# Turning old rows and scaled new rows into one sum at three boundaries of a four-stage transformer kernel

## The reference, cut to what matters

```python
def rms_norm(x, g):
    return x * rsqrt(mean(x * x, -1) + EPS) * g

def conv_ffn(x, w_up, conv_w, conv_b, w_down):        # FFN_HIDDEN = 2816
    u = x @ w_up
    c = conv_b + sum(conv_w[j] * shifted(u, j - 1) for j in range(3))   # over tokens
    g, val = split(c)
    return (gelu(g) * val) @ w_down

a = mixer(rms_norm(h, g0));     h = h + rms_norm(a, g1)
f = conv_ffn(rms_norm(h, g2));  h = h + rms_norm(f, g3)
```

## Time and profile before

| what | value |
|---|---|
| median of three runs | 1057.07 us |
| the profiled execution | 1056.94 us |
| its span in the trace | 1055.1 us |
| PE busy | 1026.9 us, 97% |
| DVE, ACT, POOL busy | 63%, 53%, 40% |
| granted PE clock, mean | 0.999 of full speed |

### The profile page before, as it was taken

How to read it: one execution, slowest core, us unless ns; L and a number is a source line. 1 busy time by engine, 2 the same in 40 slices (tenths; PEclk the granted TensorE clock), 3 DMA queues, 4 the chain that set the end, 5 groups by cost and what they waited for, 6 DMA issues and landing times.

```text
span 1055.1 us, 21644 instructions
## 1 busy us (share of the span) xinstructions
PE 1026.9 (97%) x8138; PEld 941.0 (89%) x8138; DVE 667.6 (63%) x1094; ACT 557.1 (53%) x1014; POOL 418.1 (40%) x283
## 2 busy tenths in 40 slices
PE   9999999999999999999999999999999999999997
PEld 7788699999978888699999987899999999999996
DVE  4555867767767766777676766766676555554445
ACT  5655665555564654665555556644543455554442
POOL 1000243334333443433343363865653375533331
PEclk9999999999999999999999999999999999999999
DMA  9334456566434443365655624333213245446551
GB/s 354 102 120 140 159 182 206 188 201 191 151 138 160 156 135 128 124 210 184 201 191 167 205 77 160 104 119 120 81 62 121 81 140 157 151 135 215 195 181 42
DMA packets 46284, 161.82 MB, mean 153 GB/s; under 512 B 5264, under 2 KB 6544, under 8 KB 46096
## 3 DMA queue, kind: packets, MB, share of 16 engines
q1 hardware_dynamic: 45072, 156.79, 44.7%
q0 software_dynamic: 1152, 4.19, 1.2%
HBM read 159.91 MB, written 1.05 MB: 153 GB/s over the span
## 4 chain that ended last, share of the span: by engine, by line
PE 89%; DVE 5%; ACT 2%; POOL 2%; issue 1%; DMA 0%; DVEq 0%; SPq 0%; ACTq 0%
PE work L411 13%; PE work L413 13%; PE work L412 13%; PE work L1849 9%; PE acc L411 6%; PE acc L412 6%; PE acc L413 6%; PE work L2567 4%; PE work L2579 3%; PE acc L2579 2%; PE acc L2096 1%; PE acc L2110 1%; PE acc L2112 1%; PE acc L1941 1%; PE work L1387 1%
## 5 line engine op out<-in xcount | busy, mean ns | idle before, releaser
L380 POOL TENSOR_TENSOR low<-raw,high 128x1024 fp32r<-128x1024 f32 x110 | 269.0, 2449 | 276.5 <-ACT high L367 274.0
L380 DVE TENSOR_TENSOR low<-raw,high 128x1024 fp32r<-128x1024 f32 (+1 forms) x185 | 271.0, 1473 | 147.9 <-ACT high L367 147.8
L367 ACT ACTIVATE high<-raw 128x1024 fp32r<-128x1024 f32 (+2 forms) x295 | 298.6, 1026 | 36.6 <-DMA raw<-in_w_out 23.7
L411 PE MATMUL work<-xh,high 128*128 128x256 f32 (+1 forms) x1032 | 290.0, 281 | 2.1 <-DVE v_sb L1534 1.7
L412 PE MATMUL work<-xl,high 128*128 128x256 f32 (+1 forms) x1032 | 287.9, 279 | 0.0
L413 PE MATMUL work<-xh,low 128*128 128x256 f32 (+1 forms) x1032 | 287.8, 279 | 0.0
L411 PEld LDWEIGHTS work<-xh,high 128*128 128x128 f32 (+1 forms) x1032 | 193.2, 187 | 9.0 <-issue 5.6
L412 PEld LDWEIGHTS work<-xl,high 128*128 128x128 f32 (+1 forms) x1032 | 193.3, 187 | 1.7
L413 PEld LDWEIGHTS work<-xh,low 128*128 128x128 f32 (+1 forms) x1032 | 193.3, 187 | 0.2
L1290 POOL TENSOR_TENSOR h<-gelu,cv 128x256 f32<-128x256 f32 x44 | 49.7, 1130 | 194.3 <-ACT gelu L1214 87.6
L1849 PE MATMUL work<-xh,high 128*128 128x256 f32 x256 | 76.7, 300 | 0.0
(11 more groups left out here) (402 smaller groups left out, 2172.5 us busy)
## 6 DMA issues: line engine op xcount, KB each, us to landing
raw<-in_w_ffn SPq DMA_DIRECT2D x130, 512.0 KB, 4.3
raw<-in_w_out SPq DMA_DIRECT2D x39, 512.0 KB, 4.3
raw<-in_w_att SPq DMA_DIRECT2D x32, 512.0 KB, 3.9
raw<-in_w_diff SPq DMA_DIRECT2D x31, 512.0 KB, 3.9
raw<-in_w_gdn SPq DMA_DIRECT2D x24, 512.0 KB, 4.4
raw<-in_w_mla SPq DMA_DIRECT2D x8, 512.0 KB, 3.7
raw<-in_w_gdnz SPq DMA_DIRECT2D x8, 512.0 KB, 4.0
raw<-in_w_mla SPq DMA_DIRECT2D x8, 384.0 KB, 3.3
```

The source lines that it names most:

```text
L367: act.activation(high[k][:, 0:w], raw[k][:, 0:w], ACT.Copy).then_inc(high_done[k], 1)
L380: eng.tensor_tensor(low[k][:, 0:w], raw[k][:, 0:w], high[k][:, 0:w], ALU.subtract).then_inc(low_done[k], 1)
L411: pe.matmul(out, lhs[0], rhs[0], start=start, stop=False)
```

## The change

At boundaries n = 0, 1 and 2 PE no longer turns finished rows. Right after its last product it multiplies the old `hid` rows by the identity into the PSUM tiles `work` (16 products). When the root of the new rows is known, DVE makes `share[t]`, a diagonal matrix of it (`post_share`), and PE multiplies `hn` by `share[t]`, adding into the same tiles (16 more). So the turned sum arises in PSUM while DVE adds the same into `hid`. `post_add` waits until PE has read the old rows. The split applies the channel gain at all boundaries (`pre_gain` is now 32 columns in `vec`, and three loads of a gain matrix on POOL's queue go away), block by block, with a wait for each pair.

The feed-forward stages work on raw rows as differential attention did. Their factor is made after the split (`factor_mean_dve`), PE's factor products stand ahead of the second value product of step 0, and DVE multiplies every gate and value product in PSUM by the factor (`scaled`) before ACT and DVE take its taps; the tap semaphores count three per step. DVE's order inside a step is new, and step 1 is written apart. At boundary n = 3 the diagonal of the new root multiplies `hid` on PE in place of `pre_norm`; one spin less stands ahead of it.

```diff
-    def raw_pe(pe):
+    def raw_pe(pe, n):
+        pe.wait_ge(g["const"], 48)
         for t in range(NT):
...
+            for b in range(KB):
+                last = pe.matmul(raw_turned(b)[:, t * P:(t + 1) * P], hid[:, t, b * P:(b + 1) * P], ident,
+                                 start=t == 0 and b % 2 == 0, stop=False)
+            last.then_inc(n_["turned"], 1)
+        for t in range(NT):
+            pe.wait_ge(n_["share"], 2 * (n - 1) + t + 1)
             for half in range(2):
...
+                for b in range(4 * half, 4 * half + 4):
+                    last = pe.matmul(raw_turned(b)[:, t * P:(t + 1) * P], hn[:, t, b * P:(b + 1) * P], share[t],
+                                     start=False, stop=t == 1 and b % 2 == 1)
                 last.then_inc(n_["turned"], 1)
         spin(pe, acc[:, 3, :], 1)
...
+    def post_share(dve, n, t):
+        dve.wait_ge(q_["upd"], 4 * n + 2 * t + 2)
+        dve.wait_ge(q_["root"], 2 * n + t + 1)
+        dve.tensor_scalar(share[t], ident, stat[:, 10 + t:11 + t], None, ALU.mult).then_inc(n_["share"], 1)
...
+    def post_late_dve(dve, n, p, k):
+
+        for t in range(NT):
+            for half in (1, 0):
+                post_gained(dve, n, t, half, p, k)
+            post_mean(dve, n, t)
+        post_share(dve, n, 0)
+        post_add(dve, n, 0, 0)
+        post_share(dve, n, 1)
+        post_add(dve, n, 0, 1)
...
-    def boundary_dve(dve, n, p, k):
-        post_dve(dve, n, p, k)
-        pre_dve(dve, n + 1)
+        post_add(dve, n, 1, 0)
         pre_split_dve(dve, n + 1)
+        post_add(dve, n, 1, 1)
...
+        def scaled(j, value, i):
+            bank, tap = 2 * j + value, (f[j]["g_tap"], f[j]["v_tap"])[value]
+            dve.wait_ge(used[bank], p.base[bank] + i + 1)
+            dve.tensor_tensor(W[bank][:, 0:TOK], W[bank][:, 0:TOK], factor, ALU.mult).then_inc(tap, 1)
...
         def step(i):
...
+            scaled(0, 0, i)
+            if not is0(i) and not (isinstance(i, int) and i == 1):
+                refill(split, p, 5, i - 2)
+            tapped(0, 0, i)
+            scaled(0, 1, i)
+            if not is0(i):
+                refill(split, p, 0, i)
+            tapped(0, 1, i)
+            if not is0(i):
+                refill(split, p, 1, i)
+            if is0(i) and layer == 0:
+                split(p, 5, 0)
+            scaled(1, 0, i)
+            if not is0(i) and not (is_last(i) and layer == 0):
                 refill(split, p, 4, i - 1)
...
+            tapped(1, 0, i)
+            scaled(1, 1, i)
+            if not is_last(i):
+                refill(split, p, 2, i)
+            tapped(1, 1, i)
+            if not is_last(i):
+                refill(split, p, 3, i)
...
+        refill(split, p, 0, 0)
+        refill(split, p, 1, 0)
+        factor_dve(dve, 2 * layer + 1)
         step(0)
...
+        step(1)
...
@@
-        boundary_act(act, 0, ph["mla"], 2)
+        act.wait_ge(g["const"], 48)
+        boundary_raw_act(act, 0, ph["mla"], 2)
         refill(hi_of(act), ph["mla"], 2, HEADS - 1)
+        pre_act(act, 1)
         split_high(act, ph["ffn0"], 4, 0)
-        act.wait_ge(g["const"], 48)
         ffn_act(act, 0)
...
-        boundary_dve(dve, 0, ph["mla"], 2)
+        boundary_raw_dve(dve, 0, ph["mla"], 2)
         refill(lo_of(dve), ph["mla"], 2, HEADS - 1)
+        factor_mean_dve(dve, 1)
         split_low(dve, False, ph["ffn0"], 4, 0)
         ffn_dve(dve, 0)
```

More of the change, by code:

```diff
@@ L492, in build @@
     g = sems("g", "x second_x const")
-    n_ = sems("n", "hid sq mean root hn turned xh xl gain")
+    n_ = sems("n", "hid sq mean root hn turned share xh xl")
     h = sems("h", "qkev s mx sm e p pt ptev vev pv oh ol rope roped turned turned_ev")
@@ L525, in spin, with split_seen @@
             pe.matmul(bank, ident, cst("dist"), start=True, stop=True)
+    def split_seen(n):
+        return 4 + KB * (n - 1)
+    HN_SEEN = {n: 4 * (n - 1) for n in range(1, 5)}
     def pre_pe(pe, n):
         pe.wait_ge(g["const"], 48)
[L529 to L535, removed]
+        spin(pe, W[3][:], 6)
+        for half in range(2):
+            for t in range(NT):
+                pe.wait_ge(n_["hn"], HN_SEEN[n] + t + 1)
+                for b in range(4 * half, 4 * half + 4):
+                    last = pe.matmul(raw_turned(b)[:, t * P:(t + 1) * P], hid[:, t, b * P:(b + 1) * P], diag[t],
+                                     start=True, stop=True)
                 last.then_inc(n_["turned"], 1)
-        spin(pe, acc[:, 3, :], 1)
     def cols(half):
@@ L1204, in block @@
                 bank, s = 2 * j + value, f[j]
-                act.wait_ge(used[bank], p.base[bank] + i + 1)
+                act.wait_ge((s["g_tap"], s["v_tap"])[value], 3 * (i + done) + 1)
                 if value and not (isinstance(i, int) and i + done == 0):
@@ L1245, in ffn_dve @@
         split = lo_of(dve)
-        def block(j, i):
-            for value in range(2):
-                bank, s = 2 * j + value, f[j]
-                mid, tap, c = (s["g_mid"], s["v_mid"])[value], (s["g_tap"], s["v_tap"])[value], (cg, cv)[value][j]
-                dve.wait_ge(mid, i + done + 1)
-                dve.scalar_tensor_tensor(c[:, 1:TOK], W[bank][:, 0:TOK - 1], ffn_taps(layer, i, j, value, 0, 0),
-                                         c[:, 1:TOK], ALU.mult, ALU.add).then_inc(tap, 1)
-                dve.wait_ge(tap, 2 * (i + done) + 1)
-                dve.scalar_tensor_tensor(c[:, 0:TOK - 1], W[bank][:, 1:TOK], ffn_taps(layer, i, j, value, 2, 0),
-                                         c[:, 0:TOK - 1], ALU.mult, ALU.add).then_inc(tap, 1)
-                if not (is_last(i) and j == 1):
-                    refill(split, p, bank, i)
@@ new lines, in tapped @@
+        def tapped(j, value, i):
+            bank, s = 2 * j + value, f[j]
+            mid, tap, c = (s["g_mid"], s["v_mid"])[value], (s["g_tap"], s["v_tap"])[value], (cg, cv)[value][j]
+            dve.wait_ge(mid, i + done + 1)
+            dve.scalar_tensor_tensor(c[:, 1:TOK], W[bank][:, 0:TOK - 1], ffn_taps(layer, i, j, value, 0, 0),
+                                     c[:, 1:TOK], ALU.mult, ALU.add).then_inc(tap, 1)
+            dve.wait_ge(tap, 3 * (i + done) + 2)
+            dve.scalar_tensor_tensor(c[:, 0:TOK - 1], W[bank][:, 1:TOK], ffn_taps(layer, i, j, value, 2, 0),
+                                     c[:, 0:TOK - 1], ALU.mult, ALU.add).then_inc(tap, 1)
```

186 lines of the change are left out of this document (84 added, 102 removed).

## The result

The changed kernel takes 1082.32 us (median of 4 runs, 1081.96 to 1082.75) against 1057.11 (1056.88 to 1058.06): a ratio of 1.0237, 95% interval 1.0219 to 1.0255. That is 25.2 us slower, where 6.9 were forecast. The profiled execution took 1081.96, its span is 1080.1; before it was 1055.1.

A forecast was written before the change was run, and what follows sets the result against it. PE, busy 97%, was taken to bound the kernel, with the waits at the boundaries to win. Terms 2.78 + 2.24 + 2.14 - 0.3 = +6.9 on 1056.94 gave 1063.8 us, own range 1060.5 to 1068.

The forecast's parts named there:

- Raw products at 0.22: At the first three boundaries, each product of old or new rows takes two records, 0.22 us.
- Rival (b): Boundary products take one record of 0.109 us, the price of turns; total 1055.8 us, chance 0.06.
- First and third boundary: The first feed-forward product behind each comes earlier, by 2.18 us at the first and 2.17 at the third.
- Starts: First steps of both feed-forward stages: late factor delays scalings, taps, low halves; boundary and start together +2.78 and +2.14 us.
- Rival (a): Starts of the feed-forward stages stay covered, so the kernel is not slower; 1055.8 us, chance 0.15.
- Second boundary: Ahead of differential attention: PE's 28 products of 0.22 come late where the rows were not, +2.24 us.
- Fourth boundary: Ahead of the gates' products: two diagonals replace four norms and a spin goes, -0.3 us (-0.8 to +0.7).
- At nothing: Gain loads, 24 more vec columns and four scalings a loop step (1.65 us of DVE in 16.7) cost no time.
- Rival (c): The feed-forward loops lose cover too, 0.5 us in each of 18 later steps; 1072.8 us, chance 0.09.
- The range: The forecast's own range for the whole kernel's time, 1060.5 to 1068 us.
- both starts half covered: Case at the two feed-forward starts given for the lower end of the forecast's own range, 1060.5 us.

The follow-up runs named there:

- e9: Kernel with the early value scaling, plus two spins in each of two long PE waits at the feed-forward starts; 1067.79 us.
- e4: Changed kernel, with DVE scaling the value product right behind the gate product in steps 2 to 10; 1069.79 us.
- e1: Changed kernel, with the scaling of products cut to one column in steps 2 to 10 of both feed-forward stages; 1072.43 us.
- e7: Kernel with the early value scaling, plus factor copy and scalings moved ahead of low halves in step 0, early scaling in step 1; 1063.07 us.
- e10: Kernel before, with the change at the second boundary alone; 1060.37 us (median of 10 runs).
- e11: Changed kernel, with POOL's low half of bank 3 waiting for DVE's low half of bank 5 in steps 1 to 9; 1067.63 us.
- e2: Changed kernel, with each gate product's scaling run once more into a scratch tile in steps 2 to 10; 1081.85 us.
- e3: Changed kernel, with each value product's scaling run once more into a scratch tile in steps 2 to 10; 1093.73 us.
- e8: Changed kernel with early value scaling, early factor and the old second boundary, a leftover DVE wait still in; 1062.56 us.

## Why the prediction was wrong

The direction was right, the size was not: 25 against 6.9, and the range ended at 1068. Step by step:

- **Raw products at 0.22** (two records of 0.11): right, 3.57 for 32 records. Rival (b), products at the price of turns, is out.
- **First and third boundary**, 2.18 and 2.17 gained: measured 2.06 and 2.05.
- **Starts**: the links were right but for one. Bank 2's low half frees PE at 143.41 (forecast 142.95 plus the 0.72 by which this execution was late already), POOL's low half of bank 3 at 148.79 (148.4 plus 0.72); the taps of bank 0 in stage 2 hold PE for 2.62 (2.37). What was missing is the clock behind those waits: e9 prices it at 1.55 in stage 1, the excess was 1.32. The link that failed to show is bank 3 in stage 2, forecast 1.33 late: PE waits for nothing there after the change, nor in e4, where the lower clock slows PE just ahead of it; in e9 and e1, at full clock, it waits. That this made up for part of the clock, and left an excess of only 0.85, is luck. Rival (a), cover, is out; e7 shows that the chain is the one described.
- **Second boundary**, +2.24: 2.36 after, 2.35 alone in e10.
- **Fourth boundary**, -0.3: +0.30. The turns waited 1.11 for the diagonals. The clock has no part in it: it was back at 1.00 from 652 on, and e4, where it did not fall, takes 15.45 with a wait of 1.14, against 15.11 before. In e11 the wait is 0.80 and the stretch 15.10. Not tried by itself.
- **The step that failed** stands under "At nothing": "4 scalings a step in the loops, 1.65 us of DVE in a 16.7 us step where its other work is some 12". It compares sums of busy time. But DVE's idle time in a step was not free: it is a wait inside a cycle of ACT, DVE and POOL, and that cycle already took 16.41 of the 16.69. The margin was 0.28 a step (0.21 in the second stage), and the two scalings in the cycle take 0.66. e2 and e3 show it with the same work: in the idle time 0, in the cycle 11.4. This step is 12.0 + 1.3 of the missing 18.1, the lower clock behind the wait of 3.79 included, and e4 takes 11.4 of it back by moving the two scalings out of the cycle; the rest lies in the two starts with their clock (2.2), differential attention (1.13), the start of the kernel (0.72) and the fourth boundary (0.6).
- **Rival (c)** named the place, at 0.5 a step and with a chance of 0.09, and was turned down by the same sum ("DVE has some 3 us free a step"). Its test was wrong too: "if PE waits in every step". In stage 1 PE waits in no step of the loop and pays all of it in the last. The rows to read were two POOL products a step apart, in the trace of before.
- **The range.** Its lower end, "both starts half covered", comes to 1059.8 by the prediction's own bounds and not to 1060.5; nothing hangs on it.

The 0.72 at the start is scatter between executions, not the change. The first spins took 5.48 in this profile; the profile of e2, the same up to the first feed-forward stage, has 4.48, as before has 4.47. Over all the profiles MLA ends between 112.61 and 113.97.

## What to carry to other kernels

Before costing an addition to a helper engine at nothing, measure the period of the helpers' own cycle (the same instruction, one step apart) and set it against the period of the bound engine: the margin is their difference, not the idle time. A cycle slower than the bound engine can show as no wait in the loop and as one long wait at its end, so look at the last step. Where the margin is gone, look for which of the added operations lie between a wait and what it feeds, and move those into the idle time ahead: two lines of order were worth half of what the change cost, and one wait that kept two engines from colliding was worth more.

## What the runs showed that I had not expected

- POOL's low half stops not only DVE's low halves. In stage 2's start a factor column, 128x128 from SBUF by a scalar, took 3.05 instead of 0.28. It started beside POOL's issue of a load (463.71 to 464.31) and ended at 466.85, just behind POOL's low half (464.33 to 466.76): the second row of the pair in DVE's timeline after is

```profile
463.06 0.28 DVE L612 TENSOR_SCALAR hn<-const,stat 128x128 f32<-128x128 f32 x1
463.80 3.05 DVE L612 TENSOR_SCALAR hn<-const,stat 128x128 f32<-128x128 f32 x1 [0.47 <-POOL stat L627]
```

- The clock fell behind waits from 1.71 (e8) to 4.13 (e3), but not behind each: in the kernel before it stayed at 1.00 behind one of 1.71, in e1 behind waits of 2.12, 2.31 and 2.62, and in e9 where spins left idle gaps of 0.6 and 0.8. What decides was not settled. A stall that a change adds can cost half as much again, or more, in what follows it.
- A scaling in place in PSUM (PSUM times SBUF back to PSUM, 128x256) takes 0.42, and 0.33 from its start to the next one's: as the SBUF target of the earlier trace rows.
